# Where the rows of the moving operands lie within 256 bytes, for 20,976 matmuls of 256 columns

## The reference

```python
hn = rmsnorm(x, norm_mix_g);  proj = hn @ w_in + b_in        # 2048 x 11,272
hm = mlstm_chunkwise(q, k, v, i_pre, f_pre)                  # 4 heads, a small part of the time
y_m = (norm(hm) * sigmoid(o_pre)) @ w_branch_m
y_c = (cb * causal_dwconv(cc * ch, conv_w)) @ w_branch_c
h = x + (sigmoid(gm) * y_m + sigmoid(gc) * y_c) @ w_out
u = causal_dwconv(rmsnorm(h, norm_ffn_g) @ w_up, ffn_conv_w, ffn_conv_b)   # 2048 x 11,008
h = rmsnorm(h + (silu(gate) * val) @ w_down, norm_out_g)
# second block: 16 meta tokens ahead, so 272 rows
proj = rmsnorm([meta; h]) @ w_in_2                           # pool, lru, gelu and two gates
merged = sigmoid(g_pool) * pool_mixer(v) + sigmoid(g_lru) * rg_lru(conv(v_lru)) * gelu(v_gelu)
h = h + merged @ w_out_2
h = h + square(relu(rmsnorm(h) @ mlp_w1)) @ mlp_w2           # 2048 -> 8192 -> 2048
out = rmsnorm(h)[16:]
```

## The kernel before

| | before | after |
|---|---|---|
| whi, wlo: start | 49280, 65664 | 49280, 65664 |
| a weight tile | every 512 bytes | same |
| hn: start, row | 98432, 2112 | 98624, 2304 |
| hn rows read by L459 to L461: distance modulo 256 | 64, 128, 192, 0, 64, ... by kt | 192 for all |
| act: start, row | 132224, 2048 | 135488, 2048 |
| act rows: distance | 0 for all | 192 for all |
| hn rows read by L483 and L485 | 0, 64, 128, 192, ... | 128 for all |
| lo2 rows (L484) | 224, 32, 96, 160, ... | 160, 224, 32, 96, ... |

## Time and profile before

### The profile page before, as it was taken

How to read it: one execution, slowest core, us unless ns; L and a number is a source line. 1 busy time by engine, 2 the same in 40 slices (tenths; PEclk the granted TensorE clock), 3 DMA queues, 4 the chain that set the end, 5 groups by cost and what they waited for, 6 DMA issues and landing times.

```text
span 2913.7 us, 53265 instructions
## 1 busy us (share of the span) xinstructions
PE 2790.9 (96%) x22994; PEld 2769.6 (95%) x22994; DVE 1711.9 (59%) x1725; ACT 1301.0 (45%) x1449; POOL 1.9 (0%) x14
## 2 busy tenths in 40 slices
PE   4988999999999999999989977999999999999998
PEld 4987999999999999999989977999999999999998
DVE  4544464466676466646785657755665555455554
ACT  3443454434554345434553466444444334343443
POOL 0000000000000000000000000000000000000000
PEclk9989999999999999999999988999999999999999
DMA  4443555555555555555445433555555565555653
GB/s 152 161 143 103 186 188 187 187 179 183 184 178 187 188 188 187 184 178 173 163 168 176 159 115 104 193 187 182 186 189 181 182 186 190 178 185 187 181 184 113
DMA packets 257815, 503.17 MB, mean 173 GB/s; under 512 B 10151, under 2 KB 19039, under 8 KB 257631
## 3 DMA queue, kind: packets, MB, share of 16 engines
q1 hardware_dynamic: 254592, 500.20, 52.3%
q10 hardware_dynamic: 3054, 0.55, 0.1%
HBM read 498.63 MB, written 2.10 MB: 172 GB/s over the span
## 4 chain that ended last, share of the span: by engine, by line
PE 88%; DVE 7%; ACT 3%; ACTq 1%; issue 1%; DVEq 0%
PE psum L459 27%; PE psum L461 27%; PE psum L460 27%; PE psum L483 2%; PE psum L485 2%; PE psum L484 2%; DVE wlo L1038 2%; DVE work L1066 1%; ACTq L711 1%; DVE work L1406 1%; ACT whi L725 1%; DVE misc L1452 0%; ACT misc L948 0%; DVE hn L1076 0%; ACT hn L746 0%
## 5 line engine op out<-in xcount | busy, mean ns | idle before, releaser
L1038 DVE TENSOR_TENSOR wlo<-raw,whi 128x1024 fp32r<-128x1024 f32 x952 | 1160.7, 1223 | 1020.6 <-ACT whi L725 1020.1
L725 ACT ACTIVATE whi<-raw 128x1024 fp32r<-128x1024 f32 x952 | 1004.2, 1059 | 1363.4 <-PE psum L461 1245.9
L459 PE MATMUL psum<-hn,whi 128*128 128x256 f32 x4448 | 1255.4, 282 | 37.5 <-DVE wlo L1038 23.8
L460 PE MATMUL psum<-hn,whi 128*128 128x256 f32 x4448 | 1251.8, 281 | 0.0
L461 PE MATMUL psum<-hn,wlo 128*128 128x256 f32 x4448 | 1250.4, 281 | 0.0
L459 PEld LDWEIGHTS psum<-hn,whi 128*128 128x128 f32 x4448 | 844.7, 190 | 40.4 <-DVE wlo L1038 27.4
L460 PEld LDWEIGHTS psum<-hn,whi 128*128 128x128 f32 x4448 | 844.3, 190 | 0.1
L461 PEld LDWEIGHTS psum<-hn,wlo 128*128 128x128 f32 x4448 | 844.3, 190 | 0.0
L459 PE MATMUL psum<-act,whi 128*128 128x256 f32 x2544 | 721.9, 284 | 11.0 <-DVE wlo L1038 6.8
L460 PE MATMUL psum<-act,whi 128*128 128x256 f32 x2544 | 721.3, 284 | 0.0
L461 PE MATMUL psum<-act,wlo 128*128 128x256 f32 x2544 | 721.2, 284 | 0.0
(11 more groups left out here) (207 smaller groups left out, 972.4 us busy)
## 6 DMA issues: line engine op xcount, KB each, us to landing
raw<-in_w_in SPq DMA_DIRECT2D x160, 1024.0 KB, 5.1
raw<-in_mlp_w SPq DMA_DIRECT2D x128, 1024.0 KB, 5.3
raw<-in_w_up SPq DMA_DIRECT2D x80, 1024.0 KB, 5.0
raw<-in_w_down SPq DMA_DIRECT2D x40, 1024.0 KB, 5.1
raw<-in_w_out SPq DMA_DIRECT2D x32, 1024.0 KB, 5.0
raw<-in_w_branch_m SPq DMA_DIRECT2D x8, 1024.0 KB, 5.1
raw<-in_w_branch_c SPq DMA_DIRECT2D x8, 1024.0 KB, 5.0
raw<-in_w_up SPq DMA_DIRECT2D x8, 768.0 KB, 4.3
```

What stands on the lines that cost most here:

```text
L459: mm(o, hi[:, kk, w], both[:, 0, :], start=first, stop=False)
L460: mm(o, hi[:, kk, w], both[:, 1, :], start=False, stop=False)
L725: A(whi[:, n % SLOTS, :], raw[:, n // 2 % RAW, n % 2 * HALF:(n % 2 + 1) * HALF], ACT.Copy)\
L1038: V.tensor_tensor(wlo[:, n % SLOTS, :], raw[:, n // 2 % RAW, n % 2 * HALF:(n % 2 + 1) * HALF], whi[:, n % SLOTS, :].bitcast(F32), ALU.subt ...
```

## The change

The rows of hn become 576 instead of 528 elements long (2304 bytes, nine times 256). The 256 tokens begin at column 64, the meta tokens lie in the 16 columns before it, and their low part, which had a tensor of its own, in the 16 before those. A tensor of 48 elements that nothing uses is declared ahead of hn, so that hn and all that follows move by 192 bytes more. The room comes from `ones` (128 columns instead of 256; the scan reads one column with step 0) and from the rows of the mLSTM part: three rows instead of four, declared behind `misc`. There the guard stays in `row_a`, and the denominator and what is made of it go to `row_c`.

No engine gets an instruction more or less or in another order; three have another shape or form of access: the memset of `ones`, the making of `meta_lo` and its copy into `lo2`. The kernel's lines shift by one or two.

```diff
+MAIN = 64
...
-        hn = sb("hn", [P, NT, META + 2 * T], F32R)
+        sb("gap_a", [P, 48])
+        hn = sb("hn", [P, NT, MAIN + 2 * T], F32R)
         act = sb("act", [P, NT, 2 * T], F32R)
-        meta_lo = sb("meta_lo", [P, NT, META], F32R)
-        rows4 = sb("rows4", [HEADS, 4, T])
+        meta_lo = hn[:, :, MAIN - 2 * META:MAIN - META]
         cols = sb("cols", [P, len(STAGES) * P])
         ident = sb("ident", [P, P])
-        ones = sb("ones", [P, T])
+        ones = sb("ones", [P, P])
...
-        row_a, row_b, row_c, row_guard = [rows4[:, j, :] for j in range(4)]
+        rows3 = sb("rows3", [HEADS, 3, T])
+        row_a, row_b, row_c = [rows3[:, j, :] for j in range(3)]
...
-                            mm(o, hi[:, kk, w], hn[:, kt, 0:TM], start=(kt == 0), stop=False)
+                            mm(o, hi[:, kk, w], hn[:, kt, MAIN - META:MAIN + T], start=(kt == 0), stop=False)
                             mm(o, hi[:, kk, w], lo2[:, kt, :], start=False, stop=False)
-                            last = mm(o, lo[:, kk, w], hn[:, kt, 0:TM], start=False, stop=(kt == NT - 1))
+                            last = mm(o, lo[:, kk, w], hn[:, kt, MAIN - META:MAIN + T], start=False, stop=(kt == NT - 1))
...
-                return hn[:, kt, META:META + 2 * T].rearrange("p (a t) -> p a t", t=T)
+                return hn[:, kt, MAIN:MAIN + 2 * T].rearrange("p (a t) -> p a t", t=T)
...
-            A(row_guard, row_guard, ACT.Exp, scale=-1.0).then_inc(sem("guard_ready"), 1)
+            A(row_a, row_a, ACT.Exp, scale=-1.0).then_inc(sem("guard_ready"), 1)
...
-            A(row_a, psum[0:HEADS, 4, 0:T], ACT.Abs).then_inc(sem("den_abs"), 1)
+            A(row_c, psum[0:HEADS, 4, 0:T], ACT.Abs).then_inc(sem("den_abs"), 1)
...
-            link(V.tensor_tensor_scan(row_a, ones[0:HEADS, 0:T], row_b, 0.0, ALU.mult, ALU.add))
+            link(V.tensor_tensor_scan(row_a, ones[0:HEADS, 0:1].to_broadcast([HEADS, T]), row_b, 0.0, ALU.mult, ALU.add))
...
-            V.tensor_tensor(row_guard, row_a, row_b, ALU.add).then_inc(sem("guard_sum"), 1)
+            V.tensor_tensor(row_a, row_a, row_b, ALU.add).then_inc(sem("guard_sum"), 1)
```

More of the change, by code:

```diff
@@ L602, in _ @@
             for hd in range(HEADS):
-                last = mm(psum[:, 6 + hd // 2, hd % 2 * T:(hd % 2 + 1) * T], spread_row(hd), row_a,
+                last = mm(psum[:, 6 + hd // 2, hd % 2 * T:(hd % 2 + 1) * T], spread_row(hd), row_c,
                           start=True, stop=True)
@@ L745, in high @@
                 for m in range(GW):
-                    last = A(hn[:, ds(GW * g + m, 1), META:META + T], h[:, ds(GW * g + m, 1), :], ACT.Copy,
+                    last = A(hn[:, ds(GW * g + m, 1), MAIN:MAIN + T], h[:, ds(GW * g + m, 1), :], ACT.Copy,
                              scale=gain(GW * g + m))
@@ L1074, in low_operand @@
                         t = GW * g + m
-                        dst = lo2[:, ds(t, 1), META:TM] if again else hn[:, ds(t, 1), META + T:META + 2 * T]
+                        dst = lo2[:, ds(t, 1), META:TM] if again else hn[:, ds(t, 1), MAIN + T:MAIN + 2 * T]
                         last = V.scalar_tensor_tensor(dst, h[:, ds(t, 1), :], gain(t),
-                                                      hn[:, ds(t, 1), META:META + T].bitcast(F32),
+                                                      hn[:, ds(t, 1), MAIN:MAIN + T].bitcast(F32),
                                                       ALU.mult, ALU.subtract)
@@ L1131, in setup_sums @@
                                          cols[:, g1:g1 + NT].unsqueeze(2).to_broadcast([P, NT, META]), ALU.mult))
-                    link(V.tensor_copy(hn[:, :, 0:META], meta_f))
-                    link(V.tensor_tensor(meta_lo[:, :, :], meta_f, hn[:, :, 0:META].bitcast(F32), ALU.subtract))
+                    link(V.tensor_copy(hn[:, :, MAIN - META:MAIN], meta_f))
+                    link(V.tensor_tensor(meta_lo, meta_f, hn[:, :, MAIN - META:MAIN].bitcast(F32), ALU.subtract))
                     ve.wait_ge(sem("gate_b_loaded"), 16)
@@ L1200, in _ @@
             ve.wait_ge(sem("guard_ready"), 1)
-            link(V.tensor_tensor(row_a, row_a, row_guard, ALU.max))
-            link(V.reciprocal(row_a, row_a))
-            link(V.tensor_tensor(row_b, row_a, row_a, ALU.mult))
+            link(V.tensor_tensor(row_c, row_c, row_a, ALU.max))
+            link(V.reciprocal(row_c, row_c))
+            link(V.tensor_tensor(row_b, row_c, row_c, ALU.mult))
             ve.wait_ge(sem("squares_used"), HEADS)
@@ L1207, in _ @@
             link(V.reciprocal(row_b, row_b))
-            V.tensor_tensor(row_a, row_a, row_b, ALU.mult).then_inc(sem("factor_made"), 1)
+            V.tensor_tensor(row_c, row_c, row_b, ALU.mult).then_inc(sem("factor_made"), 1)
             ve.wait_ge(sem("factor_copied"), 1)
@@ L1310, in _ @@
             ve.wait_ge(sem("up_cleared"), 2)
-            V.tensor_copy(lo2[:, :, 0:META], meta_lo[:, :, :].bitcast(F32)).then_inc(sem("lo2_made"), 1)
+            V.tensor_copy(lo2[:, :, 0:META], meta_lo.bitcast(F32)).then_inc(sem("lo2_made"), 1)
             def up(first, base, tiles=GW):
```

## The result

| | before | changed |
|---|---|---|
| median | 2918.2 us (2917.5 to 2919.0, 4 runs) | 2873.97 us (2864.8 to 2880.6, 4 runs) |
| ratio | | 0.9846 (95%: 0.9822 to 0.9869) |
| profiled execution, and its span | 2915.5, 2913.7 us | 2872.5, 2870.7 us |

The kernel is 44 us faster; 102 us were forecast. The time lies in the stated range, near the 2868 us of rival 2. New as well is the spread: the runs of before lie within 1.5 us, those of the changed kernel 16 us apart.

A forecast was written before the change was run, and what follows sets the result against it. The prediction took the pitch between matmul starts on PE as the bound, set by the rows' distance from the weights. Stretch gains of 103.7 us less 1.8 gave 101.9 us, so 2813.6 profiled and 2816.6 us median; range 2808 to 2907.

The forecast's parts named there:

- rival 2: Pitch drawn anew at each restart; 117.8 ns after the sums in up_0 and mlp1_0 loses 51 us: 2868 us; 17%.
- the price of one matmul: Ordinary matmuls where PE doesn't wait: 4.35 ns gained on hn (117.65 to 113.3), 6.7 ns on act (120.0 to 113.3).
- the fast course: All hn and act rows at distance 192 bytes from the weights settle at 113.3 ns per ordinary matmul; 50%.
- the wide stages: lru_in and pool_in, 1536 matmuls of 272 columns: plus or minus 1.5 us, taken as a cost of 0.8 us.
- the two sums: Sums of squares in up_0 and mlp1_0, named as restarts after which matmuls might fall to 117.8 ns, losing 51 us.
- the 272 blocks of twelve: Blocks at distance 192 in the kernel before; nearly all reach 113 ns within five matmuls, cited against a regular 117.8.
- the prediction's sum: Gains of all stretches, 103.7 us less 1.8, so 101.9 us; profiled execution 2813.6 us, median 2816.6 us.
- the 3.0 us added from profiled execution to median: Whole kernel: median of the runs taken as 3.0 us above the profiled execution, giving 2816.6 from 2813.6 us.
- Rival 1: Fixed distance 192 runs at 117.8 ns as in up_3; gain only 12 us, 2906.5 us; 18%.
- Rival 3: Distance is not the cause; 113 ns comes from alternating places and vanishes when all are alike: 2918 us; 8%.
- Rival 4: Any constant distance settles at 120 ns as act does; hn loses 31 us, 2950 us; 5%.
- the place of a row could not matter: Ordinary matmuls: the skill's rule of two independent ports would make the change worth nothing; 120.0 against 113.3 ns disagreed.

The follow-up runs named there:

- e5: Changed kernel with all hn and act rows at distance 112 bytes from the weights instead of 192; 2817.12 us, ratio 0.9655.
- e3: Changed kernel with a gap of 64 bytes instead of 192, so all rows lie at distance 64; 2894.94 us, ratio 0.9915.
- e10: Kernel before, with act alone moved to distance 112 and hn left as it was; 2873.81 us, ratio 0.9850.
- e11: e5 with act back at distance 0, so only hn rows are at 112; 2864.66 us, ratio 0.9818.
- e1: Separate kernel without the reference's computation: 72 matmuls at sixteen distances, eight starts each; 112 took 113.3 ns at all starts, 192 took 113.3 or 117.8.
- e9: Like e1, but high weights, low weights or both also moved; both moved by 64, rows at distance 112 took 113.3 ns; both moved by 112, 120.0 and 118.3.
- e2: Changed kernel without the gap: padded hn rows, but hn and act at distance 0; 2947.65 us, ratio 1.0102.
- e7: Kernel of e1 at 100 to 124 and 184 to 200 bytes in steps of 4, six starts each; 112 took 113.3 ns at all six, 192 at two.
- e6: Changed kernel with one more wait, for ScalarE's root, after the sum of squares in up_0 and in mlp1_0; 2841.87 us, ratio 0.9750.

## Why the prediction was wrong

**What bounds the kernel, and the price of one matmul: right.** The pitch from start to start was the quantity to read, and both its values stand in the changed kernel as in the earlier trace rows. Nothing else became the bound.

**The step that failed: that the fast course holds in all stretches that PE fills.** The prediction set hn at 113.3 and act at 113.3 throughout and gave that 50%. In the profiled execution about 11,600 ordinary matmuls ran at 117.8 instead: some 1030 in qkvo, 1580 from the sum in up_0 into down_0, 370 in up_3 and down_2, 8600 from pool_mix to the end. At 4.5 ns each that is 52 us. The measure is the profiled execution of e5, 2817.1 us, where the same stages all run at 113.3: the changed kernel's took 2872.5, 55 us more. Of the 3 us beside the 52, 2 lie in the wide stages: by kt their matmuls ran at 125.4 to 126.7 ns, as a mean 126.1, against 124.7 in e5. That is 0.8 ns more than before, where 0.5 were allowed for.

**Rival 2 described what happened.** It had the mechanism (the course is drawn at a restart and then held; e3 has one change without a restart), and 2868 us; I gave it 17%. It named restarts after the two sums, and behind both the slow course ran. But it had too few: hold-ups of 0.2 to 1.6 us draw as well, and the one in pool_mix had drawn the slow course 2480 matmuls ahead of the sum in mlp1_0, while qkvo was slow and down_0 behind its hold-up fast. That its 2868 us lie 6 us from the median is partly luck, since the draws differ from execution to execution. The rows to weigh it were there: of the two starts in the earlier trace rows one was slow, and up_3 in the earlier trace rows was slow through two groups. I counted the 272 blocks of twelve as many witnesses for the fast course. They were one witness: nearly all enter distance 192 the same way, out of the same regular pattern, so they say nothing of how often another entry ends there.

**The sum was right for a kernel that holds the course.** e5 has every long stretch at 113.3 and takes 2817.1 us, where the prediction's sum gives 2816.6. That the two agree within 1 us is luck in part. For the profiled execution the sum gives 2813.6, and e5's took 2817.1, 3.5 more; the 3.0 us added from profiled execution to median did not show in e5, where the two are the same. The parts are less exact too: alone, act gains 44 us (e10) where the prediction's terms for it make 49, and hn 53 us (e11) where they make 55; and the wide stages, for which 0.8 us were taken off, ran at 124.7 ns in e5 (124.2 to 125.4 by kt), 0.6 less than before.

**Rival 1** (117.8 throughout) held for some 11,600 matmuls of the changed kernel; a kernel that has it almost throughout is e3, at 64, with 2904 us in the profiled execution. **Rival 3** is excluded by e1 and e9. **Rival 4** claimed 120 ns for any constant distance; its time came at distance 0 alone (e2, 2947.7 us), and at 192 and 112 the pitch was 113.3 or 117.8.

**The rule of the Trainium skill** ("TensorE: Matmul & The Clock Gate", "Step-by-step: what each phase is for"), by which loading the next weights takes no SBUF read bandwidth from the running matmul, led the prediction to "the place of a row could not matter". The runs disagree with that for these fp32r matmuls: e2 and e5 differ by 130 us in places alone. That weight loads and moving reads hinder each other is my reading of it, and not shown. It rests on e9, where moving weights and row together by 64 or 192 keeps the pitch at 0, 112 and 192, and with one set of weights moved no row gave 113.3; no run here takes the weight loads away.

**What stays open:** what in a restart picks the course. At 192, sums gave the slow one at 5 of 5 starts in e1 and e7, long waits the fast one at 3 of 3, short waits the fast one at 5 of 6, and one and the same hold-up in down_1 went both ways. e9 adds three of each where the weights were moved by 0, 64 or 192: slow after the sum, fast after the short wait. Open too is what changed the course in e3 with no restart, and why moving weights and row by 112 together changes the pitch.

## What to carry to other kernels

Where PE is never idle, read the distance between starts for each place that an operand can have, not the mean duration; 6% of a matmul's time hung on the address of its row. A pitch that follows one transition many hundred times is one observation, and a regular slow stretch at the same place is worth as much: ask of each value how it was entered. Before laying out a kernel by such a value, measure each candidate place with several kinds of start; the place that gives its value at all starts (112 here) is worth more than one that gives the same value at most, and its spread between executions (1.3 us against 29) tells which of the two one has.

## What was not expected of the hardware

- For fp32r matmuls of 128x256 with a weight load each, the pitch at full clock takes one of several values between 113.3 and 123.3 ns as a mean of 30, by where the row lies against the weights, in steps as fine as 4 bytes: 108, 112 and 116 gave 120.0, 113.3 and 121.5 to 121.8.
- At one distance two values can hold, each for thousands of matmuls (2280 at 113.3 and, from the sum in mlp1_0 on, some 6000 at 117.8 in the changed kernel). A hold-up of 0.18 us moved it from one to the other, and at distance 64 it moved once with none (e3). In e6, behind an added wait of 1.3 us, up_0 ran at 113.3, where both traces without it had 117.8.
- Nine executions of one program differed by 29 us (2851.4 to 2880.6) at granted clocks of 0.979 to 0.981; the two traces among them have stages at different pitches.
